# Six norms of a fused two-block transformer kernel worked in halves of 256 tokens

## What is computed

```python
def rms_norm(x, gain):
    y = x * lax.rsqrt(jnp.mean(x * x, axis=-1, keepdims=True) + EPS)
    return y * gain

hn = rms_norm(h, g_ffn1[l]) * (1.0 + sc1) + sh1
h = h + 0.5 * (1.0 + gt1) * swiglu(hn, w_ffn1_in[l], w_ffn1_out[l])
hn = rms_norm(h, g_mix[l]) * (1.0 + sc2) + sh2
proj = hn @ w_mix_in[l]
...
h = h + (1.0 + gt2) * mixed
hn = rms_norm(h, g_ffn2[l]) * (1.0 + sc3) + sh3
```

## Time and profile before

| | us |
|---|---|
| median of 3 runs | 2789.36 |
| lowest and highest | 2786.97, 2793.34 |
| the profiled execution | 2792.05 |
| its span, first to last instruction | 2790.3 |
| TensorE busy by the profile | 2690.6 (96%) |
| VectorE, ScalarE, GpSimd busy | 1489.0, 965.1, 206.2 |

### The profile page before, as it was taken

How to read it: one execution, slowest core, us unless ns; L and a number is a source line. 1 busy time by engine, 2 the same in 40 slices (tenths; PEclk the granted TensorE clock), 3 DMA queues, 4 the chain that set the end, 5 groups by cost and what they waited for, 6 DMA issues and landing times.

```text
span 2790.3 us, 42160 instructions
## 1 busy us (share of the span) xinstructions
PE 2690.6 (96%) x17668; PEld 2212.2 (79%) x17668; DVE 1489.0 (53%) x1850; ACT 965.1 (35%) x1472; POOL 206.2 (7%) x284
## 2 busy tenths in 40 slices
PE   6999999999999999999999999999999999978998
PEld 5888878787888887888877787888878777768787
DVE  6555575765565434333356754333355565775644
ACT  3222233623222233222335433222233544533332
POOL 3000000220000000000000410000000000043000
PEclk9999999999999999999999999999999999988999
DMA  7566552102556322233222102232233331240222
GB/s 296 188 215 218 172 187 91 65 3 98 211 192 223 126 95 89 86 103 105 83 91 79 33 32 83 89 107 90 91 101 127 104 106 68 87 116 4 69 94 76
DMA packets 53370, 313.41 MB, mean 112 GB/s; under 512 B 7617, under 2 KB 7745, under 8 KB 24929
## 3 DMA queue, kind: packets, MB, share of 16 engines
q1 hardware_dynamic: 41760, 236.65, 24.9%
q0 software_dynamic: 11456, 74.55, 7.9%
HBM read 302.69 MB, written 2.20 MB: 109 GB/s over the span
## 4 chain that ended last, share of the span: by engine, by line
PE 91%; DVE 5%; DMA 2%; ACT 1%; issue 1%; POOL 0%; SPq 0%; DVEq 0%; ACTq 0%
PE ps L971 18%; PE ps L972 18%; PE ps L973 18%; PE ps L1259 6%; PE ps L1260 6%; PE ps L1261 6%; PE ps L2130 1%; PE ps L2114 1%; PE ps L2127 1%; PE ps L1526 1%; PE ps L1528 1%; PE ps L1527 1%; DMA ada_first<-in_ada 1%; DVE w_lo L947 1%; PE ps L1341 1%; PE ps L1996 1%
## 5 line engine op out<-in xcount | busy, mean ns | idle before, releaser
L971 PE MATMUL ps<-hn_hi,w_hi 128*128 128x512 f32 x1440 | 564.9, 392 | 16.6 <-DVE hn_lo L920 16.6
L972 PE MATMUL ps<-hn_lo,w_hi 128*128 128x512 f32 x1440 | 563.9, 392 | 0.0
L973 PE MATMUL ps<-hn_hi,w_lo 128*128 128x512 f32 x1440 | 563.8, 392 | 0.0
L947 DVE TENSOR_TENSOR w_lo<-w_raw,w_hi 128x2048 fp32r<-128x2048 f32 (+2 forms) x227 | 467.9, 2061 | 163.0 <-ACT w_hi L940 162.9
L940 ACT ACTIVATE w_hi<-w_raw 128x2048 fp32r<-128x2048 f32 (+2 forms) x227 | 390.7, 1721 | 94.0 <-PE ps L1261 90.6
L971 PEld LDWEIGHTS ps<-hn_hi,w_hi 128*128 128x128 f32 x1440 | 272.8, 189 | 75.5 <-issue 18.4
L1259 PE MATMUL ps<-hn_hi,w_hi 128*128 128x512 f32 x776 | 316.3, 408 | 15.6 <-DVE spare L1454 7.0
L972 PEld LDWEIGHTS ps<-hn_lo,w_hi 128*128 128x128 f32 x1440 | 272.8, 189 | 56.8
L973 PEld LDWEIGHTS ps<-hn_hi,w_lo 128*128 128x128 f32 x1440 | 272.5, 189 | 56.9
L1260 PE MATMUL ps<-hn_lo,w_hi 128*128 128x512 f32 x776 | 307.8, 397 | 0.0
L1261 PE MATMUL ps<-hn_hi,w_lo 128*128 128x512 f32 x776 | 307.3, 396 | 0.0
(11 more groups left out here) (461 smaller groups left out, 3518.3 us busy)
## 6 DMA issues: line engine op xcount, KB each, us to landing
w_raw<-in_up SPq DMA_DIRECT2D x88, 1024.0 KB, 4.8
ada_w<-in_ada POOLq DMA_DIRECT2D x64, 1024.0 KB, 5.1
w_raw<-in_down SPq DMA_DIRECT2D x64, 704.0 KB, 4.1
w_raw<-in_mix_in SPq DMA_DIRECT2D x20, 1024.0 KB, 4.8
w_raw<-in_dsa_in SPq DMA_DIRECT2D x18, 1024.0 KB, 5.2
w_raw<-in_merge SPq DMA_DIRECT2D x16, 768.0 KB, 4.2
ada_first<-in_ada SPq DMA_DIRECT2D x8, 1024.0 KB, 12.3
w_raw<-in_mix_out SPq DMA_DIRECT2D x8, 1024.0 KB, 4.9
```

What stands on the lines that cost most here:

```text
L947: dve.tensor_tensor(w_lo[:, slot, 0:size], w_raw[:, slot, 0:size], w_hi[:, slot, 0:size].bitcast(F32), ALU.subtract).then_inc(w_lo_ready, 1)
L971: pe.matmul(bank, wh, x_hi[:, k], start=(k == 0), stop=False)
L972: pe.matmul(bank, wh, x_lo[:, k], start=False, stop=False)
L973: return pe.matmul(bank, wl, x_hi[:, k], start=False, stop=(k == K - 1))
```

## The change

Norms 1 to 6 are worked in two halves of 256 tokens. The last `down` piece (or last `mix_out` piece) computes its products for tokens 0 to 255 and then for 256 to 511; the sums, root, reciprocal and spreading of the first half stand between the products of the second. The first piece of the next phase also runs by halves, each with its inner tiles in order. In the norm, low parts of odd tiles go to GpSimd; where there is a shift, ScalarE writes each odd tile a second time, unrounded, into a new buffer `hn_x` for GpSimd. The split of the second new piece on ScalarE stands inside the first half of the norm, in two parts. One `ada` piece moves from beside the last `down` piece ahead of norm 1 to behind norm 1. The loads of `ada` pieces 40 and on stand behind GpSimd's part of norm 2. Three semaphores are merged into others.

The core of the diff:

```diff
+        def low_ready(n, hf, j):
+            if not halved(n):
+                return hn_ready, j + 1
+            at = KD * (n - 1) + KD // 2 * hf + j // 2 + 1
+            return (hn_pool, at) if j % 2 else (hn_ready, KD + at)
+        def norm_pool(pool, n):
+            for hf in range(2):
+                for j in range(1, KD, 2):
+                    norm_low(pool, n, hf, j, shift).then_inc(hn_pool, 1)
+        def tail_ffn_pe(pe, n):
...
+            for hf in range(2):
+                for k in range(HALF):
+                    wh, wl = w_hi[:, slot, k * P:(k + 1) * P], w_lo[:, slot, k * P:(k + 1) * P]
+                    last = split_products(pe, main[slot][hf][:, cols(hf)], wh, wl, act_hi[:, k, cols(hf)], act_lo[:, k, cols(hf)],
+                                          k == 0, k == HALF - 1)
+                    if hf == 0 and k == 5:
+                        pe.wait_ge(sq_added, SQ_ADDS * n)
+                        early_sums_pe(pe, n, rstd[:], True)
+                    if hf and k == 2:
+                        tail_sums_pe(pe, n, 0)
+                    if hf and k == 5:
+                        tail_spread_pe(pe, n, 0)
+                if hf == 0:
+                    last.then_inc(tail_done, 1)
+                    pe.wait_ge(sq_ready, squares_before(n) + KD - 1)
+                    early_sums_pe(pe, n, norm_squares(n)[:, (KD - 2) % 2], False)
+        def first_halves_pe(pe, n, p, narrow):
...
+            for hf in range(2):
+                for k in range(KD):
+                    pe.wait_ge(*low_ready(n, hf, k))
+                    for t in range(2):
+                        last = split_products(...)
+                    if hf == 0 and k == 3:
+                        tail_sums_pe(pe, n, 1)
+                    if hf == 0 and k == 6:
+                        tail_spread_pe(pe, n, 1)
+        def norm_halves_act(act, n, shift):
+            def high(hf, j):
+                act.wait_ge(hn_tmp, hn_before(n, hf) + j + 1)
+                x = tmp[:, j % 2, cols(hf)]
+                if shift is None:
+                    last = act.activation(hn_hi[:, j, cols(hf)], x, ACT.Copy)
+                else:
+                    last = act.activation(hn_hi[:, j, cols(hf)], x, ACT.Identity, bias=shift[:, j:j + 1])
+                    if j % 2:
+                        if n > 1 or hf or j > 1:
+                            act.wait_ge(hn_pool, KD * (n - 1) + KD // 2 * hf + j // 2)
+                        last = act.activation(hn_x[:, cols(hf)], x, ACT.Identity, bias=shift[:, j:j + 1])
+                last.then_inc(hn_hi_ready, 1)
...
+            tail_root_act(act, n, 0)
+            high(0, 0)
+            high(0, 1)
+            tail_evac_act(act, n, 1)
+            high(0, 2)
+            act.wait_ge(piece_done, tail_of(n)[1] + 1)
+            split(0)
+            high(0, 3)
+            tail_square_act(act, n, 1)
+            high(0, 4)
+            high(0, 5)
+            tail_root_act(act, n, 1)
+            high(0, 6)
+            high(0, 7)
+            split(1)
+            for j in range(KD):
+                high(1, j)
+        def norm_halves_dve(dve, n, shift):
+            def scaled(hf, j):
+                if j >= 2:
+                    dve.wait_ge(*low_ready(n, hf, j - 2))
+                dve.scalar_tensor_tensor(tmp[:, j % 2, cols(hf)], h[:, j, cols(hf)], norm_gain[:, j:j + 1], small[2 * hf][:, cols(hf)],
+                                         ALU.mult, ALU.mult).then_inc(hn_tmp, 1)
+            tail_rstd_dve(dve, n, 0)
+            for hf in range(2):
+                dve.wait_ge(norm_spread, norm_count(n, hf))
+                for j in range(0, KD, 2):
+                    scaled(hf, j)
+                    if hf == 0 and j == 2:
+                        tail_update_dve(dve, n, 1)
+                    scaled(hf, j + 1)
+                    norm_low(dve, n, hf, j, shift).then_inc(hn_ready, 1)
+                    if hf == 0 and j == 4:
+                        tail_rstd_dve(dve, n, 1)
@@ mix_dve
             norm_dve(dve, own, 3 * l + 1, gains[:, l, 1], mods(l, 4), mods(l, 3))
+            if l == 0:
+                dve_ada(dve, ADA_BEFORE_MIX - 1)
```

More of the change, by code:

```diff
@@ L625, in dsa_swap_sp, with halved, tail_of, tails_before @@
                 sp.dma_start(t[a:a + H], x[b:b + H]).then_inc(dsa_swapped[m % 2], 16)
+        def halved(n):
+            return 1 <= n <= 3 * LAYERS
+        def tail_of(n):
+            if n % 3 == 2:
+                return "mix", start_of["mix_out", (n // 3, 0)] + KD // 2 - 1
+            return "ffn", start_of["down", (2 * (n // 3) + (0 if n % 3 else -1), 1)] + KD - 1
+        def tails_before(n):
+            return sum(3 if m % 3 == 2 else 1 for m in range(1, n))
+        def squares_before(n):
+            return sum((KD + 2 if m % 3 == 2 else KD + 1) if m else KD for m in range(n))
+        def hn_before(n, hf=0):
+            return (KD + 2 * KD * (n - 1) if n else 0) + KD * hf
+        def low_ready(n, hf, j):
[3 more added lines that the diff above has]
+            return (hn_pool, at) if j % 2 else (hn_ready, KD + at)
+        def norm_count(n, hf=0):
+            return 2 * n + hf if n else 1
+        def cols(hf):
+            return slice(hf * T // 2, (hf + 1) * T // 2)
+        def blocks(hf):
+            return range(hf * NB // 2, (hf + 1) * NB // 2)
+        def norm_low(eng, n, hf, j, shift):
+            eng.wait_ge(hn_hi_ready, hn_before(n, hf) + j + 1)
+            hi, low, x = hn_hi[:, j, cols(hf)].bitcast(F32), hn_lo[:, j, cols(hf)], tmp[:, j % 2, cols(hf)]
+            if shift is not None and j % 2:
+                x = hn_x[:, cols(hf)]
+            if shift is None or j % 2:
+                return eng.tensor_tensor(low, x, hi, ALU.subtract)
+            return eng.scalar_tensor_tensor(low, x, shift[:, j:j + 1], hi, ALU.add, ALU.subtract)
         @block.sync
@@ new lines, in early_sums_pe, with tail_spread_pe @@
+        def early_sums_pe(pe, n, squares, first):
+            for hf in range(2):
+                for b in blocks(hf):
+                    pe.matmul(small[1 + 2 * hf][:, b:b + 1], squares[:, b * P:(b + 1) * P], ones[:, 0:1],
+                              start=first and b == blocks(hf)[0], stop=False, skip_group_check=True)
+        def tail_spread_pe(pe, n, hf):
+            pe.wait_ge(norm_rooted, norm_count(n, hf))
+            for b in blocks(hf):
+                last = pe.transpose(small[2 * hf][:, b * P:(b + 1) * P], roots[:, b:b + 1].broadcast_to([P, P]), ident[:])
+            last.then_inc(norm_spread, 1)
@@ L883, in norm_act @@
         def norm_act(act, n, shift, last=False):
+            if halved(n):
+                norm_halves_act(act, n, shift)
+                return
             if n == 0:
@@ L995, in up @@
                 def up(i, odd):
+                    if halved(n) and half == 0 and isinstance(i, int) and i == 0:
+                        first_halves_pe(pe, n, p0, False)
+                        return
                     def ready(k):
@@ L1031, in up @@
                     s = (p0 + odd) % 2
-                    split_act(act, *ahead(p0, HALF, WIDE, i, odd))
+                    if not (isinstance(i, int) and i == 0 and half == 0 and f):
+                        split_act(act, *ahead(p0, HALF, WIDE, i, odd))
                     if f == 1 and half == 0 and isinstance(i, int) and i == 0:
@@ L1104, in down @@
                     split_dve(dve, *ahead(p1, KD, TALL, i, odd))
-                    if d_ada:
+                    if d_ada and not (half and i == KD - 1):
                         dve_ada(dve, d0 + i)
```

233 lines of the change are left out of this document (165 added, 68 removed).

## The result

| | before | changed |
|---|---|---|
| median, us | 2791.97 (7 runs) | 2805.22 (7 runs) |
| lowest and highest | 2786.97, 2793.42 | 2800.66, 2810.69 |
| the profiled execution, its span | 2792.05, 2790.3 | 2804.45, 2802.7 |

The changed kernel is **slower by 0.51%**: the ratio is 1.0051, with a 95% interval of 1.0041 to 1.0062. The forecast was 2798.5, with 2783 to 2817 as its range.

What follows compares the result with a forecast made beforehand. TensorE, busy 96%, was taken as the bound, losing time at six norms; there a 2.27 us three-engine loop would replace the gap. Window changes sum to +9.1 on 2792.05: 2801.2, or 2798.5 as a median, range 2783 to 2817.

Steps and rivals of the forecast that it cites:

- The loop: In each norm with a shift, VectorE scale, two ScalarE writes and GpSimd: 2.27 us per pair, 18.1 where 11.6 stood.
- The six windows: Per norm, last output tile's first product to second new piece's first product: 182.6 us together before, forecast +9.1.
- The product of 256: TensorE's half-width product in tails and first pieces: taken at 0.128 us, between bounds 0.114 and 0.214.
- Norm 4's order: At norm 4's end, three small VectorE operations let GpSimd go first; split ends at 31.4, +3.7 on 27.7.
- Behind the norm its cover is gone: Norm 1's moved ada piece, 2 x 1.28 us, no longer hidden beside the tail; window 33.1, +5.0 on 28.0.
- At most about 55 us: Most that could be won at all six norms by removing idle time and slow-clock products.
- the three slower cases: Chance of a slower kernel, 0.54: main case (0.52) less its quarter below +5.6, low clock, unhidden weight load.
- GpSimd at 0.92: Bound on the forecast sum if GpSimd's low part takes 0.92 us instead of 0.71: +16.
- The clock stays low: Rival: short products in the first piece keep TensorE's clock low, each norm 2 to 4 later; +25, 2814, chance 0.15.
- The weight load is not hidden: Rival: a product of 256 costs 0.19 us, the length of a weight load; +46, 2835, chance 0.03.
- A shorter loop: Rival: the lower bounds together in the norm, GpSimd's queue being no obstacle; -6, 2783, chance 0.20.
- The halves pay in full: Rival: TensorE alone bounds the norm, GpSimd and ScalarE ahead of it; -30, 2759, chance 0.10.

Runs made afterwards that it cites:

- Experiment 2: Changed kernel, but the scale of an odd tile waits for ScalarE's last read of tmp, not GpSimd; 2794.35 us, ratio 1.0006 to the kernel before.
- experiment 1: Changed kernel with all low parts on VectorE, none on GpSimd, and hn_x not written; 2791.33 us, ratio 0.9999 to the kernel before.
- experiment 8: Changed kernel with the second piece's ScalarE weight split moved back behind the norm; 2816.34 us, ratio 1.0080 to the kernel before.
- experiment 9: Changed kernel plus one wait: VectorE's work behind each norm waits for GpSimd's last low part; 2806.61 us, ratio 1.0051 to the kernel before.
- experiment 3: Changed kernel with the moved ada piece put at the end of the list instead of behind norm 1; 2804.09 us, ratio 1.0047 to the kernel before.
- 5: Changed kernel with all low parts on VectorE and the ada piece at the end of the list; 2784.39 us, ratio 0.9975 to the kernel before.
- 6: Changed kernel with odd scales not waiting for GpSimd, last low part on VectorE, ada piece later; 2783.10 us, ratio 0.9970 to the kernel before.
- experiment 7: Changed kernel, GpSimd only on tiles 1, 3, 5 of half 1, odd scales free, ada piece later; 2780.47 us, ratio 0.9961 to the kernel before.
- experiment 4: Changed kernel with only the low part of tile 7 of half 1 moved to VectorE; 2801.35 us, ratio 1.0035 to the kernel before.

## Why the prediction was right

**The loop.** "That is 2.27 us for a pair of half tiles": measured 2.27 in the second half of norms 1 to 5, and 1.79 in norm 6, which has no `hn_x`. It held because its terms did: scale 0.478 (taken 0.48), `hn_hi` 0.505 (0.51), `hn_x` 0.494 (0.51), GpSimd alone 0.73 (0.71). Experiment 2 shows that this loop is the main cost: 10.5 us without VectorE's wait alone, of the 14.8 without GpSimd's part (experiment 1). One sign of it failed. TensorE was to stand for GpSimd's `hn_lo` "six times and more in a norm", "at nearly every pair"; the trace lists four such waits in each of norms 1 to 5, and one in norm 6.

**The six windows**, as predicted and as measured: 33.1 and 32.3, 34.0 and 35.4, 30.9 and 30.2, 31.4 and 31.8, 34.0 and 33.9, 28.5 and 28.5; together +9.1 in the forecast and +9.5. Of the 6.7 us between forecast and median, 2.6 are the kernel before, whose median was 2789.36 in the three runs shown and 2791.97 in seven, 0.4 the windows, 2.9 lie outside them, and the rest is that the changed kernel's median lies 0.8 above its profiled execution. That the windows' sum came within 0.4 us is luck: 2.7 us of half clock, which the forecast had at nothing, stand against terms that were too long. Part by part:

- **The product of 256** was taken at 0.128 from transposes; it follows the next every 0.120. A `down` tail has 66 of them: 0.5 too long. The eight records of sums take 0.78 (taken 0.9). In norm 3 the first scale starts at 8.7 and not 9.2, half 1 at 18.5 and not 19.1, and the window ends at 30.2 and not 30.9.
- **The first product behind a wait** holds the next one back for 0.22 instead of 0.12 (from 1078.57 in experiment 8). I had no such term. It is 0.1 at each wait, and on the path it counts once, at the norm's end.
- **Norm 4's order was wrong.** "GpSimd goes first and the split ends at 31.4": the three small operations take 0.2 each, the split started at 1444.36 and GpSimd at 1444.48, and by 0.12 us VectorE won. The window was 31.8 by the other way round, with 0.8 of half clock in it that the forecast doesn't have. Its own terms give 27.9 + 0.71 + 2.29 = 30.9 for the end of the split, not 31.4. That the sum still came near is chance: two operations that are ready together and exclude each other need about the same time in either order, and norm 4 of experiment 9 ends at 30.9 with GpSimd first.
- **Norm 1**: 32.3 for 33.1. Its two `ada` reductions took 1.28 and 1.74, the second since GpSimd was at work (1.15 for its own). "Behind the norm its cover is gone" holds, but its price in this window depends on who else is there: 0.8 us beside GpSimd (experiment 3), 2.4 without (from 1 to 5).
- **Norm 2**: 1.4 longer than predicted. The granted clock there was 0.95 and not 1.00, which is 3.4 us at half the clock, 1.7 of delay. The forecast counts every product of that norm at full clock, and that was not true. TensorE's products in the tail of norm 2 are the same in all these kernels, and the clock of its window is 0.95 in the changed one and in experiments 2, 3, 5 and 6, but 1.00 in the others; what decides it stays open.

**Sums that don't come out.** "At most about 55 us" doesn't follow from its terms: 182.6 less four times 18.4 and twice 21.8 is 65. Likewise the three slower cases add up to 0.57 (0.39, 0.15 and 0.03) and not 0.54. "GpSimd at 0.92" in the bounds has no row; alone it took 0.73.

**Whole or partial exclusion.** The row alone gave "perhaps 0.4" for GpSimd's wait, the rule 1.5, and I charged 1.5. The measured 2.15 against 0.73 is 1.4, and 2.76 is 2.0 where GpSimd came right behind. Experiment 2 has the mirror image in norm 4: the split is second, takes 2.74 instead of 2.29, and ends 2.15 after GpSimd. By the Trainium skill (SBUF — State Buffer, "Who interferes with whom") an operation of VectorE with two SBUF inputs and one of GpSimd that reads SBUF lock each other out until the whole instruction is over; the trace agrees but for some 0.15 us, with 0.73 and 2.76 for the same shape.

**What was missing: 3 us outside the windows.** The edit was thought to end at the second piece. The stretch between norms 1 and 2 is 2.6 longer: the clock is at half for 3.4 us right behind norm 1 and again near 467, where the kernel before has one such stretch, near 462 (+1.7), and TensorE waits 3.5 for `d_bt` instead of 2.9. Between 5 and 6 there are 1.5 more, with 3.4 us of half clock at 1723.9 behind the window; between 4 and 5 it is 0.9 less. The half clock of the kernel before lies inside the windows, that of the changed one partly behind them. Why it comes in one norm and not in another isn't settled by these runs: norms 3 and 5 both ended on a wait of 1.8 us, norm 5 was followed by half clock, and norm 3 kept 1.00.

**The rivals.** *The clock stays low* didn't come: the windows' clock is 1.00 in four norms, 0.97 and 0.95 in the others, 2.7 us where that rival had 2 to 4 in each. The Trainium skill (TensorE: Matmul & The Clock Gate, "Why this matters for your kernels") fears an oscillating clock with thin products; products of 256 with full weights, twelve of 0.120 in every 2.27 us, did not show it in norm 3 (1.00 in its window); in norm 2 the clock fell once, for 3.4 us at 679.4, among products of 256. *The weight load is not hidden* fell with 0.120, under the 0.19 of a load. *A shorter loop* fell with 2.27. *The halves pay in full* is what experiment 7 goes towards: 27.3 and 30.6 us where that rival had 24 and 28.

## What to carry to other kernels

Before a helper engine goes into a loop, draw the loop through all its waits, those on buffer reuse among them: here VectorE alone needs 1.86 us for what took 2.27 with GpSimd's help, and 1.58 where the helper reads a copy and VectorE doesn't wait for it. When a piece of work leaves a covered place, or two operations that exclude each other meet, price the pair and not the piece: in the window of norm 1 the same `ada` piece was worth 0.8 us in one neighbourhood and 2.4 in the other. And before two kernels are compared window by window, look at the granted clock in each: 2.7 us of what experiment 4 seemed to win was clock.

## What the runs showed of the hardware

- A VectorE subtraction with two SBUF inputs and a GpSimd subtraction share next to no time. GpSimd's operation of 0.73 was written as 2.15 and 2.76 behind a split of 2.29 that had started 0.71 and 0.12 earlier; it ended 0.58 and 0.59 after the split. The other way round, a split that started 0.15 behind GpSimd took 2.74 (experiment 2) and ended 2.15 after it. An `ada` reduction on VectorE grew from 1.28 to 1.74 behind GpSimd. A lead of 0.11 us was enough to be first.
- Products of 256 columns with a fresh 128x128 weight load each follow every 0.120 us, and wide ones every 0.2275. Half of a wide one is 0.114, so the load, written as 0.19, costs at most 0.006 at that width.
- A wait of 2.6 us ahead of a piece was followed by 3.4 us at half the clock, 1.5 us into the piece (experiment 8), a delay of 1.7 which shows up neither as idle time nor in the window that ended on the wait. A wait of 1.8 us was followed by half clock in norm 5 of the changed kernel and not in norm 3.
